# A chunked recurrence in a Trainium2 kernel: the last step's terms accumulate in the chain's banks, and a transposed factor is computed by matmuls

## What the kernel computes

```python
def wkv_scan(r, w, k, v, kk, a, s0, reverse):
    def step(S, inp):
        r_t, w_t, k_t, v_t, kk_t, a_t = inp
        sa = jnp.einsum("bhvk,bhk->bhv", S, kk_t)
        S = (S * w_t[:, :, None, :]
             - sa[..., None] * (kk_t * a_t)[:, :, None, :]
             + v_t[..., None] * k_t[:, :, None, :])
        return S, jnp.einsum("bhvk,bhk->bhv", S, r_t)
    s_fin, o = lax.scan(step, s0, xs, reverse=reverse)

def rwkv7_mixer(...):
    oc_f, sc_f = scan_direction(con, 0, s0, False)
    oc_b, sc_b = scan_direction(con, 1, s0, True)
    ol_f, _ = scan_direction(lat, 0, sc_f, False)
    ol_b, _ = scan_direction(lat, 1, sc_b, True)
    y = rwkv7_readout(ol_f + ol_b, ...)       # group norm, bonus, gate, output projection
```

## Time and profile before

| | |
|---|---|
| median of three runs | 2525.03 us |
| profiled execution: span from first to last instruction | 2537.7 us |
| TensorE busy in the span | 86%, 25764 matmul instructions |
| VectorE, ScalarE, GpSimd busy | 53%, 45%, 27% |
| mean granted TensorE clock (1 is 2.4 GHz) | 0.939 |
| the recurrence: first transpose to last chain | 507 to 1211 us |

### The profile page before, as it was taken

How to read it: one execution, slowest core, us unless ns; L and a number is a source line. 1 busy time by engine, 2 the same in 40 slices (tenths; PEclk the granted TensorE clock), 3 DMA queues, 4 the chain that set the end, 5 groups by cost and what they waited for, 6 DMA issues and landing times.

```text
span 2537.7 us, 59405 instructions
## 1 busy us (share of the span) xinstructions
PE 2172.6 (86%) x25764; PEld 1625.2 (64%) x25764; DVE 1354.0 (53%) x2324; ACT 1152.3 (45%) x1933; POOL 681.8 (27%) x412
## 2 busy tenths in 40 slices
PE   8799999288888888887789999996888987898888
PEld 2587777067766767676667666663666665666666
DVE  1357878434444455454345666664356663466752
ACT  2466767233333334343335454543355553355552
POOL 0334443200001011011433222222443332433332
PEclk9899999589998899998989999997999998999998
DMA  7215453652332222312313111111222221222222
GB/s 259 71 59 170 132 159 117 179 147 78 100 105 75 68 63 51 78 43 71 135 56 108 51 50 54 55 42 43 90 75 83 67 67 66 67 79 76 63 67 67
DMA packets 156163, 221.37 MB, mean 87 GB/s; under 512 B 84480, under 2 KB 109312, under 8 KB 155136
## 3 DMA queue, kind: packets, MB, share of 16 engines
q1 hardware_dynamic: 144800, 174.32, 22.4%
q0 software_dynamic: 9952, 40.11, 5.2%
q10 hardware_dynamic: 1152, 3.15, 0.3%
HBM read 164.84 MB, written 42.21 MB: 82 GB/s over the span
## 4 chain that ended last, share of the span: by engine, by line
PE 59%; DVE 15%; ACT 11%; issue 8%; POOL 4%; DMA 2%; SPq 0%; ACTq 0%; DVEq 0%; POOLq 0%
PE ps L257 8%; PE ps L259 7%; PE ps L258 7%; PE ps L1337 3%; PE ps L543 3%; PE ps L1327 2%; PE ps L1352 2%; PE ps L2257 2%; PE ps L396 2%; PE ps L2794 2%; PE ps L2217 1%; PE ps L2771 1%; PE ps L1202 1%; ACT p L2277 1%; DVE s L921 1%
## 5 line engine op out<-in xcount | busy, mean ns | idle before, releaser
L242 POOL TENSOR_TENSOR wbl<-wb,wbh 128x1024 fp32r<-128x1024 f32 x128 | 309.4, 2418 | 661.3 <-ACT wbh L237 657.5
L257 PE MATMUL ps<-hTh,wah 128*128 128x512 f32 (+1 forms) x512 | 180.6, 353 | 17.3 <-POOL wal L242 10.8
L257 PE MATMUL ps<-hT2h,wbh 128*128 128x512 f32 x416 | 180.2, 433 | 10.7 <-POOL wbl L242 10.5
L258 PE MATMUL ps<-hTl,wah 128*128 128x512 f32 (+1 forms) x512 | 174.9, 342 | 0.0
L259 PE MATMUL ps<-hTh,wal 128*128 128x512 f32 (+1 forms) x512 | 174.7, 341 | 0.0
L257 PE MATMUL ps<-hT1h,wbh 128*128 128x512 f32 (+1 forms) x432 | 169.0, 391 | 3.1 <-POOL hT1l L2398 3.1
L344 POOL TENSOR_TENSOR ro<-ro 128x256 f32<-128x256 f32 (+1 forms) x12 | 11.9, 993 | 586.7 <-DVE ro L328 586.7
L237 ACT ACTIVATE wbh<-wb 128x1024 fp32r<-128x1024 f32 x128 | 134.6, 1052 | 69.5 <-PE ps L1936 43.5
L259 PE MATMUL ps<-hT2h,wbl 128*128 128x512 f32 x416 | 164.5, 395 | 0.0
L258 PE MATMUL ps<-hT2l,wbh 128*128 128x512 f32 x416 | 163.9, 394 | 0.0
L242 POOL TENSOR_TENSOR wal<-wa,wah 128x1024 fp32r<-128x1024 f32 x34 | 102.2, 3008 | 219.2 <-ACT wah L237 219.2
(11 more groups left out here) (410 smaller groups left out, 5612.6 us busy)
## 6 DMA issues: line engine op xcount, KB each, us to landing
wb<-in_w_in SPq DMA_DIRECT2D x56, 512.0 KB, 3.5
s_str_dram<-s POOLq DMA_DIRECT2D x48, 576.0 KB, 8.7
wm<-in_ada SPq DMA_DIRECT2D x48, 512.0 KB, 4.5
bkv<-s_str_dram SPq DMA_DIRECT2D x96, 192.0 KB, 3.3
wa<-in_rw_in SPq DMA_DIRECT2D x34, 512.0 KB, 4.4
wb<-in_da_in SPq DMA_DIRECT2D x32, 512.0 KB, 3.4
ARI<-s_str_dram SPq DMA_DIRECT2D x96, 128.0 KB, 3.4
wb<-in_w_out SPq DMA_DIRECT2D x16, 512.0 KB, 3.5
```

The source lines that it names most:

```text
L242: e.tensor_tensor(self.lo[:, n % 2], self.raw[:, n % 3], self.hi[:, n % 2].bitcast(F32), ALU.subtract).then_inc(self.K.s.w_lo, 1)
L257: e.matmul(z, wh[:, k, :], hi[:, k, a:b], start=k == 0, stop=False)
L258: e.matmul(z, wh[:, k, :], lo[:, k, a:b], start=False, stop=False)
```

## The change

It has three parts. (1) Step 15 of the inverse writes its terms into banks 6 and 7, where the chain adds G and Q times the state to them; `H`, the product with the identity, ScalarE's copies and VectorE's separate add go. The chain's output is taken out once per unit by one instruction with all partitions (`dve_output`), and `S` by one per step. (2) `pe_update` multiplies D up by 16 more matmuls into the other half of the same banks, ScalarE copies both halves at once, and the transposes go. (3) The modulation moves to a class `Tiled`: four column tiles of 128 columns on 2 rows each, into bank 0 in each second unit, and one matmul with a constant `sel` in place of four to turn it.

```diff
@@ class Tiled(Modulation)
+    def pe_row(self, e, c, out):
+        for kk in range(4):
+            i = 4 * c + kk
+            e.wait_ge(self.sem[i % 4], self.in0[i % 4] + 16 * (i // 4 + 1))
...
+            for d in range(2):
+                for t in range(4):
+                    m = e.matmul(out[32 * t:32 * t + 2, :], K.s0[:, 2 * kk + d, :], rows[:, d, 128 * t:128 * t + 128],
+                                 start=kk + d == 0, stop=kk + d == 4)
+            m.then_inc(K.s.mod_mm, 1)
+    def act_row(self, e, c, src):
+        e.wait_ge(self.K.s.mod_mm, self.mm0 + 4 * c + 4)
+        e.activation(self.mrow[:, :], src, ACT.Copy).then_inc(self.K.s.mod_row, 1)
+    def pe_turn(self, e, c, out):
+        self.row_out(e, c)
+        return e.matmul(out, self.mrow[:, :], self.K.C("sel"), start=True, stop=True)
@@ pe_prepare
-        if self.chunks(u):
-            self.mod.pe_chunks(e, self.chunks(u))
+        if u in range(1, 12, 2):
+            self.free(e, i + 5)
+            self.mod.pe_row(e, u // 2, ps[:, 0, 256:384])
         yield
         self.free(e, self.x_use(u))
+        if u in range(1, 12, 2):
+            self.mod.row_out(e, u // 2)
@@ pe_level
-        if l > 1:
-            for d, h in QUADS:
-                e.transpose(ps[:, x + h, 256 + 128 * d:384 + 128 * d], D[:, h, 128 * d:128 * d + 128], K.ident)
@@ pe_update
+        if l < 5:
+            for d, c in QUADS:
+                for h, q in TILES:
+                    E = self.E1[half(h), 2 * d + q, c, :] if l == 1 else old[half(h), q, blk64(4 + 2 * d + c)]
+                    m = e.matmul(ps[half(q), x + h, blk64(4 + 2 * d + c)], self.Y[half(h), l - 1, c, blk64(2 * d + q)], E,
+                                 start=True, stop=True)
@@ pe_invert, start of a unit
         if u >= 2:
-            e.wait_ge(*self.iv_at(u - 2, a=12))
-            e.wait_ge(*self.iv_at(u - 2, v=8))
+            e.wait_ge(*self.iv_at(u - 2, v=7))
@@ pe_invert, step 15
-        e.wait_ge(*self.iv_at(u, v=7))
+        if u:
+            e.wait_ge(s.ch_s, 2 * u)
+            e.wait_ge(s.ch_o, u)
         for d, c in QUADS:
-            q = blk64(2 * d + c)
+            q, o = blk64(2 * d + c), self.place(u, d, c)
             for p, j in TILES:
-                e.matmul(ps[half(j), x + p, q], self.bkl[half(p), w, 1, 2 * d + c, j, :], self.vax[half(p), w, 0, 2 * d + c, j, :], start=True,
-                         stop=False)
+                e.matmul(ps[half(j), 6 + p, q], self.bkl[half(p), w, 1, 2 * d + c, j, :], self.vax[half(p), w, 0, 2 * d + c, j, :],
+                         start=(d, c) == (0, 0), stop=False, skip_group_check=True)
...
@@ act_invert
-            e.activation(self.DE[:, u % 2, 1 - l % 2, :, 0:256], banks[:, :, 0:256], ACT.Copy).then_inc(a, 1)
+            e.activation(self.DE[:, u % 2, 1 - l % 2], banks, ACT.Copy).then_inc(a, 1)
             yield
-            e.wait_ge(*self.iv_at(u, mm=2 * l + 3))
-            e.activation(self.DE[:, u % 2, 1 - l % 2, :, 256:512], banks[:, :, 256:512], ACT.Copy).then_inc(a, 1)
...
-        m = e.activation(self.H[:, u % 2], banks[:, :, 0:256], ACT.Copy)
...
@@ dve_invert
-            if l > 1:
-                e.wait_ge(*self.iv_at(u, a=2 * l - 1))
...
-            m = e.tensor_tensor(o, o, banks[:, :, 256 + 128 * d:384 + 128 * d], ALU.add)
...
@@ pe_chain
-            for j in range(2):
-                e.matmul(ps[half(j), 6 + j, 0:256], I[half(j), half(j)],
-                         H[half(j)].rearrange("x p (q t) -> x p q t", t=64)[:, :, self.at_step(h), :], start=True,
-                         stop=False)
...
+                    e.matmul(ps[half(j), 6 + p, blk64(2 * d + c)], G[half(j), p, blk64(2 * d + c)],
+                                 S[half(j), sc, 2 * p + d, :], start=False, stop=False, skip_group_check=True)
@@ dve_chain
-            for j in range(2):
...
+            e.tensor_tensor(S[:, 1 - sc].rearrange("x (p d) v -> x p d v", p=2),
+                            ps[:, 6:8, 0:256].rearrange("x p (q v) -> x p q v", v=64)[:, :, self.at_step(h), :],
+                            pc.unsqueeze(3).to_broadcast([128, 2, 2, 64]), ALU.mult).then_inc(s.ch_s, 1)
+            if h == 1:
+                self.dve_output(e, u)
@@ dve_output, new
+    def dve_output(self, e, u):
...
+        if self.first(u, 0):
...
+            e.tensor_copy(o, new).then_inc(s.ch_o, 1)
+        else:
+            e.wait_ge(s.ch_o, u)
+            e.tensor_tensor(o, o, new, ALU.add).then_inc(s.ch_o, 1)
```

More of the change, by code:

```diff
@@ L34 @@
 _n = 0
-for _name, _w in (("ident", 128), ("ones", 128), ("blk", 128), ("eps", 8)):
+for _name, _w in (("ident", 128), ("ones", 128), ("blk", 128), ("eps", 8), ("sel", 8)):
     CCOLS[_name] = (_n, _w)
@@ L1122, in __init__ @@
         self.iv = [(s.iv_mm0, s.iv_a0, s.iv_v0), (s.iv_mm1, s.iv_a1, s.iv_v1)]
-        self.adds = [sum(not self.first(x, d) for x in range(u) for d in range(2)) for u in range(25)]
     @staticmethod
     def turn(u):
-        return u // 4 * 2 - 2 if u in (4, 8, 12) else None
+        return u // 2 - 1 if u in range(2, 13, 2) else None
     @staticmethod
@@ L1143, in tile, with place @@
         return (FWD, BWD)[d][u % 6]
+    def place(self, u, d, c):
+        low = 0 if self.tile(u, 0) < self.tile(u, 1) else 1
+        return blk64(4 + 2 * (d ^ low) + c)
     def first(self, u, d):
@@ L1194, in pe_prepare @@
             self.free(e, self.turn_use[u])
-            for x in range(2):
-                m = self.mod.pe_turn(e, c + x, ps[:, x, 0:8])
-            m.then_inc(s.pp_mm, 1)
+            self.mod.pe_turn(e, c, ps[:, 0, 0:8]).then_inc(s.pp_mm, 1)
         self.free(e, i)
@@ L1280, in dve_prepare @@
             e.wait_ge(s.pp_mm, self.turn_use[u] + 1)
-            for x in range(2):
-                self.mod.dve_out(e, self.turn(u) + x, ps[:, x, 0:8])
+            self.mod.dve_out(e, self.turn(u), ps[:, 0, 0:8])
             if u == 12:
@@ L1451, in act_invert @@
         yield
-        e.wait_ge(*self.iv_at(u, mm=15))
-        if u >= 2:
-            e.wait_ge(s.ch_mm, 2 * (u - 1))
-        m = e.activation(self.H[:, u % 2], banks[:, :, 0:256], ACT.Copy)
-        for d in range(2):
-            if self.first(u, d):
-                n = self.tile(u, d)
-                if u >= 12 and u % 6 == 0 and d == 0:
-                    e.wait_ge(*self.use[self.ro_use[2 * (u // 6 - 2) + 1]])
-                m = e.activation(self.group(u)[:, :, 128 * n:128 * n + 128], banks[:, :, 256 + 128 * d:384 + 128 * d],
-                                 ACT.Copy)
-        m.then_inc(a, 1)
         yield
@@ L1497, in dve_invert @@
         yield
-        e.wait_ge(*self.iv_at(u, a=12))
-        if u:
-            e.wait_ge(s.ch_o, 2 * self.chained)
-            e.wait_ge(*self.iv_at(u - 1, v=8))
-        later = [d for d in range(2) if not self.first(u, d)]
-        for d in later:
-            n = self.tile(u, d)
-            o = self.group(u)[:, :, 128 * n:128 * n + 128]
-            m = e.tensor_tensor(o, o, banks[:, :, 256 + 128 * d:384 + 128 * d], ALU.add)
-        if later:
-            m.then_inc(v, 1)
-        else:
-            e.nop().then_inc(v, 1)
         yield
@@ L1583, in dve_chain @@
             e.memset(S[:, 0], 0.0).then_inc(s.s_set, 1)
+    def dve_output(self, e, u):
+        s = self.K.s
+        lo, hi = sorted(self.tile(u, d) for d in range(2))
+        o = self.group(u).rearrange("x p (n t) -> x p n t", t=128)[:, :, lo:hi + 1:hi - lo, :]
+        new = self.K.psum[:, 6:8, 256:512].rearrange("x p (d t) -> x p d t", d=2)
+        if self.first(u, 0):
+            if u >= 12 and u % 6 == 0:
+                e.wait_ge(*self.use[self.ro_use[2 * (u // 6 - 2) + 1]])
+            e.tensor_copy(o, new).then_inc(s.ch_o, 1)
+        else:
+            e.wait_ge(s.ch_o, u)
+            e.tensor_tensor(o, o, new, ALU.add).then_inc(s.ch_o, 1)
     def none_chain(self, e, u):
```

103 lines of the change are left out of this document (47 added, 56 removed).

## The result

The changed kernel is **slower**: 2550.98 us (2546.09 to 2552.39) against 2526.66 us for the kernel before (four runs), a ratio of 1.0086 (95% interval 1.0064 to 1.0108). The forecast was 2491 us, 1.4% faster.

A forecast was written before the change was run, and what follows sets the result against it. The prediction took TensorE's instruction supply as the near limit: plain -2, modulation -3, readout -20, ends -9, together -34 us, profiled 2537.7 to 2504, median 2491 us; own range 2472 to 2510, eight in ten 2447 to 2538.

The forecast's parts named there:

- one block ahead, about 3.4 us each, 4.5 us while the transfers run: TensorE's instruction supply in the recurrence: blocks of some 253 instructions, only one fetched ahead, at these spacings.
- 25.8 us. Everything else fits under that: Plain stages: 6.8 blocks set 25.8 us for 26.06, hiding TensorE's savings and engine waits; -2 us over seven.
- Rival B: Supply costs more than it hides, 3.67 us a quiet block, and the clock falls oftener: +12, 2537 us; chance 0.18.
- Modulation: Six stages with modulation: 7.1 blocks at supply pace plus 0.5 us of waits, 27.5 for 27.95 us each; -3 us.
- Readout stages: Eight stages with a readout or behind one: 20 of 23.8 us of waits for output adds go; -20 us.
- rival C: Readout stages: L1368 takes over the waits, the rest stays, or with B halfway; 2515 to 2530 us; chance 0.12.
- The ends: Recurrence's start and end: shorter level paths, faster last chain, H and step 15's wait for QG gone; -9 us.
- 1.4 us a stage, 34 us in 24 stages, if TensorE's own pace counts: TensorE work saved in the recurrence: 0.9 us a stage from identity products, 0.5 from transposes.
- Rival A: Supply is no limit, gaps come from transfers alone, so TensorE's savings count: -79, 2446 us; chance 0.15.
- D: Rival on the recurrence's clock: matmuls instead of transposes keep it up, up to 20 us more, 2470 us; chance 0.05.
- The two signs: Recurrence: the prediction is wrong if blocks come closer than 3 us or plain stages exceed 27 us.

The follow-up runs named there:

- The bursts: Two runs (e4, e7): the kernel before with 1024 more small matmuls, 64 or 96 columns wide, at the recurrence's end; blocks averaged 3.77 and 3.61 us.
- e9: Kernel before plus 13 four-column matmuls, results unread, at the end of each of four inverse updates a stage: 1.0269 of before.
- e3: Kernel before with only the modulation's part of the change (column tiles in place of wide rows): 0.9997 of before.
- e2: Changed kernel with the inverse's transposes, two-piece ScalarE copies and wait counts restored; last step's terms and modulation stay changed: 0.9901 of before.
- e12: The kernel of e2 run again, on the same chip as e11: 2510.95 us, 0.9917 of before.
- e11: e2 with eight pairs of preparation products merged into 128-column matmuls, both results copied by VectorE before the next product: 2492.81 us, 0.9835 of before.
- e7: Kernel before plus 1024 independent matmuls of 96 columns at the recurrence's end on TensorE: 14 quiet blocks took 50.51 us.
- e4: Kernel before plus 1024 independent matmuls of 64 columns (16 blocks) at the recurrence's end on TensorE: the burst took 64 us.
- e6: Kernel before plus two full 256-column matmuls, results unread, at the end of each of four inverse updates a stage: 1.0238 of before.
- e13: Changed kernel plus two full 256-column matmuls ahead of each of four updates a stage: 1.0181 of before.
- e14: Changed kernel plus 13 four-column matmuls ahead of each of four updates a stage: 1.0339 of before.
- e1: Kernel before with only the inverse's part of the change (16 more matmuls an update, no transposes, one ScalarE copy): 1.0176 of before.

## Why the prediction was wrong

**The limit was seen, and priced at its best case.** The step that failed is this one: "one block ahead, about 3.4 us each, 4.5 us while the transfers run", and with it the plain stage of 6.8 blocks at "25.8 us. Everything else fits under that". 3.4 us was the spacing in the densest stretch of the rows, taken as the rate. The bursts gave 3.61 and 3.77 on the average in quiet and 6 beside transfers. With 3.61 to 3.77 the prediction's own sums give 26.6 to 27.3 us for a plain stage (27.75 measured) and 28.5 to 29.2 for a modulation stage (29.5 measured). For these thirteen stages that is +7 to +16 us, where -5 was forecast and +21 measured: the rate is most of the error.

The second half of the step is unsound too: a stage's blocks were summed and compared with a stage's length, as if blocks could be stored. Only one is ahead (the 68 us without a packet, above). A dense run of groups uses it up in about 2 us and then stops, whatever the stage needs on average, so the sum is a lower bound at best. By it, with 3.61 to 3.77, a plain stage of the kernel before needed 24 us and took 26.06, room for half a block more. Yet e9, with 0.8 of a block and 2 us of execution more to a stage, had plain stages of 29.0 us where the sum says 26.6 to 27.3.

What happened in each class of stages, from the views by stretch and the waits in the same stretches (us; the lengths and busy times are sums over the rows above and over the earlier trace rows):

| stages | length | TensorE busy | "issue" | waits on engines |
|---|---|---|---|---|
| six with modulation | 167.7, then 176.8 | 147.1, then 132.9 | 10.8, then 39.6 | 9.5, then 4.4 |
| seven plain | 182.5, then 194.2 | 155.4, then 148.1 | 16.5, then 40.3 | 9.5, then 5.7 |
| eight with a readout or behind one | 249.1, then 237.8 | 207.3, then 185.5 | 11.6, then 21.7 | 29.6, then 29.6 |

**Rival B had the mechanism and the threshold** (from 3.5 us a block on), with 0.18 and at 2537 us, 14 below the result. Its own measured number, 3.67 us in the earlier trace rows, was the better one to take. The text had it and used 3.4. (B also counted 1 us a stage for a falling clock; the granted clock of the recurrence is 0.93 before and after.)

**Modulation, -3 forecast, +9 measured.** The same error: 1.0 block more a stage, and "issue" up by 29 us. The modulation's own part is not to blame: e3 shows it at 0.9997. Its column tiles did save TensorE time (busy -7.5 us) and gained nothing.

**Readout stages, -20 forecast, -11 measured, and not by the mechanism forecast.** The 20 us were to be waits that go. L1408 has no wait for `oT` any more, as forecast (20.8 us of it lay in these stages). But here L1413 waits 7.9 us for `E`, L1243 6.4 for `modc` and L1376 9.0 for `DE`, so that all waits on engines are 29.6 us as before: no wait was saved on balance. That is rival C's mechanism in full, though not its time. What made the stages shorter is TensorE's own work, busy 22 us less, of which 10 came back as "issue". In e2, without the inverse's part, they took 231.5 us (230.6 in e12), 18 less than before, again with as many waits (29.1 us) and with TensorE busy 15.5 us less. That is near the forecast 20 by luck, since the work saved was not in that term. The inverse's part took 6 of it back.

**The ends, -9 forecast, -0.5 measured**, +5.3 at the start and -5.8 at the end, up to the first matmul behind the last chain. That a level's path is shorter there was argued from durations; at the start, where dense groups of two inverses and a preparation meet, blocks are missing as well: "issue" is 8.8 us there, 1.0 before.

**What came true**: TensorE's own work. It was to fall by 34 us (and up to 15 in the modulation), and its busy time in the recurrence fell by 49. In the chain that pays: e2 against e3 has 24.6 us less busy time and 24.4 less recurrence (at 0.60 the busy time is 15 of them; the waits on engines, 73.6 and 64.7 us, are 9 more). "1.4 us a stage, 34 us in 24 stages, if TensorE's own pace counts" was right in its size; the chain's 0.9 came through in e2, the inverse's 0.5 was bought with 0.8 of a block.

**Rival A** (supply no limit, 2446 us) is refuted by the bursts, and D by nothing, but the clock did not rise as it says: its rows lie between 0.87 and 0.96, where the earlier trace rows had 0.88 to 0.98. The two signs that were to show the forecast wrong were blocks closer than 3 us and plain stages above 27 us; the second came. The sum for a plain stage has a slip of 0.1 us (4.5 x 3.4 is 15.3), which changes nothing.

## What to carry to other kernels

Count TensorE's instructions as well as its time, where groups of small matmuls follow each other: a block of 256 instructions took 3.5 to 4.0 us to arrive here, so 128 matmul instructions that execute faster than that stop the engine, and replacing few instructions by many cheap ones can cost more than it saves. Look for "issue" gaps inside groups, take a measured average for the rate and never the best interval, and compare it with the densest run of groups as well as with the mean of a stage. Where such gaps are, look for edits that give the same product in fewer, wider instructions: the one tried here (e11) gained 18 us, together with a handover that it saved, and on the changed kernel 4 us, not clear of the noise.

## What the runs showed of the hardware

- TensorE's instruction blocks: 256 instructions, 3.47 to 4.02 us apart with DMA at most 3% busy (3.77 on average when they execute in 2.09 us, 3.61 when in 2.87), and 6.21 and 5.93 us with DMA 91 and 93% busy (one interval each, e7 and e4). The packet itself takes 0.9 us.
- No more than one block is fetched ahead: 68 us without a packet (kernel before, 452 to 520 us) in which TensorE ran 256 instructions and waited 31.6 us for a transfer.
- A 64x64 matmul instruction costs no less with four columns than with 64: 19 ns each in e9 (47 us of busy time for 2496; 26 of them in 0.44 us, 926.43 to 926.87 us, are 17 ns), 16 ns in the burst of 64 columns (2.09 us for 128), 22 ns with 96 (2.87 us).
- Two full 128x256 fp32 matmuls behind 64x64 groups, four matmul instructions, take 1.06 us in e6's timeline (932.00 us to the next group at 933.06), where 0.55 was expected.
- Two pairs of prices, each solved from two runs: 2.1 us a block and 0.60 us for a us of execution in the kernel before (e6, e9), 2.65 and 0.26 in the changed one (e13, e14). The first pair gives e1, e3 and the changed kernel within 3 us and misses e2 and e12 by 8 and 5. This is a fit, not a mechanism, and an average over stages with different limits: of e1's 30.7 us, 12.7 lie in the six modulation stages, 8.4 in the seven plain ones, 9.5 in the two ends and 0.1 in the eight with a readout or behind one, where as many blocks were added to a stage.
